# A hand-ordered opening: c spread by DMA, the norm's sums taken per token, GpSimd out, loads reordered, and the first two matmul passes split by features

## The chip, the core and the metric

The kernel runs on one NeuronCore of a Trainium2 chip. The metric is device microseconds (us) of one launch; lower is better. The engines run their own instruction streams and meet at semaphores: TensorE (PE: matmuls, and weight loads as PEld), VectorE (DVE), ScalarE (ACT), GpSimd (POOL), and SyncE (SP), which here only issues DMAs.

## The reference, cut to what matters

A transformer block with conditioning from a vector, then two more layers. Only the very beginning matters here: two token sets of 256 (x and ctx), their modulation vectors, the first norm and the first half of the first feed-forward (D = 1024, D_FF = 2816):

```python
mod_lat = silu(c) @ w_mod + b_mod            # 9 pieces of 1024: shift, scale, gate, ...
mod_ctx = silu(c_ctx) @ w_mod + b_mod
h  = modulate(rms_norm(x,  norm1_g), ml[0], ml[1])    # h * (1 + scale) + shift
hc = modulate(rms_norm(ctx, norm1_g), mc[0], mc[1])
a, b = split(h @ ffn1_w_in)                  # the first matmuls; then silu(a) * b, @ ffn1_w_out
# ... attention, conv, a second feed-forward, an mLSTM / stick-breaking layer, a pooling layer
```

## The kernel before

Tokens lie transposed: `X[128, 8, 512]` holds feature k*128+p on partition p, ctx in columns 0 to 255 and x in 256 to 511. Every matmul is three matmuls: weights and tokens are split into a high part (`WH`, `XH`) and a rest (`WL`, `XL`), and high*high, rest*high and high*rest are summed in PSUM (L758 to L760). Weights come in chunks of 512 KB into a ring of six slots `W`; SP issues the loads of `plan.loads` in one fixed order, each as soon as the slot's last reader is done (L692 to L701). Per chunk ACT writes `WH` (L1140) and DVE writes `WL` (L1471); that is a `split` step.

A class `Plan` writes one list of steps, and each engine walks this list in order and does its part of every step. A `gemm` is one pass: 256 output columns of a weight matrix, two chunks of four features each (`ck` steps, 24 matmuls of 512 columns each), into two of four PSUM tiles; the passes "fa1" and "fb1" of one column pair go together (silu(a) * b). `start()` writes the opening, the steps ahead of the first pass:

- `cb`: PE spreads c and c_ctx over the partitions, a matmul with one row of ones (L786), and ACT writes their silu to `AC0` and `AC1` (L1147).
- `mp`: one 128-feature piece of the scale row, a product and a sum along 1024 elements on DVE for each of the two vectors (L1522). Eight pieces are wanted before the last features are normed.
- `mm`, `mt`: two features pairs' worth (256 values) of the shift row on PE (L795, eight matmuls), copied out by ACT (L1153), turned by PE (L802), stored by DVE as `MOD`, and `AM` = (1 + scale) * gain with it (L1487, L1489).
- `st`, `sr`: the sums of squares: eight squares of 128x512 on ACT (L985), added up by POOL (L955), then a matmul with ones (L724), a square root on ACT (L1162), a reciprocal on DVE (L1497); POOL then writes `XR` = X times that row (L960).
- `fn`: for two features k and both token sets, the tokens' high and low parts: DVE multiplies and adds (L1507), ACT rounds (L995), DVE takes the rest (L1330).

The loads stand in the order scale 0, scale 1, shift 0 (two loads), scale 2, scale 3, shift 1, and so on, and then the passes. The first pass takes features 0 to 7, then the second does.

## Time and profile before

| | us |
|---|---|
| median of 3 runs (1452.12 to 1455.38) | 1454.88 |
| the profiled execution | 1454.74 |
| its span, first to last instruction | 1452.9 |
| TensorE busy in the span | 1351.9 (93%) |
| VectorE busy | 925.9 (64%) |
| ScalarE busy | 644.9 (44%) |
| GpSimd busy | 45.6 (3%) |

Busy time is an average over stages with different limits, so the opening is read by itself: first in stretches of time, then instruction by instruction on each engine. The granted clock is TensorE's, as a share of 2.4 GHz (1.00) with 1.2 GHz as its lower level (0.50). A float32 matmul shows as two records each with its own weight load; a "half" below is one of them.

### The profile page before, as it was taken

Reading aid. Unit: us, or ns where it says so; the run is one execution under the profiler, and the core shown is the slowest. Engines: PE = TensorE matmul, PEld = TensorE weight load, DVE = VectorE, ACT = ScalarE, POOL = GpSimd, SP = SyncE. Lnnn points to the kernel's source line nnn. Section 1 sums busy time; section 2 is a strip of 40 time slices with the busy share of each in tenths; the row PEclk is TensorE's granted clock in tenths of the full one; section 3 lists DMA queues with packets and bytes.
Section 4 is the critical chain, followed back from the end, with each engine's and each line's share of the span. In section 5 each row is a group of like instructions: output and inputs, shape, how many; then the busy total and the mean of one; then the engine's idle time right before and its main releaser. Section 6 shows DMA issues by size and latency. Waiting matters only on the chain.

```text
span 1452.9 us, 22846 instructions
## 1 busy us (share of the span) xinstructions
PE 1351.9 (93%) x9116; PEld 1212.2 (83%) x9116; DVE 925.9 (64%) x1459; ACT 644.9 (44%) x1005; POOL 45.6 (3%) x42
## 2 busy tenths in 40 slices
PE   4599999999997999999989999899999999889996
PEld 1378888888885789999989999779899998879996
DVE  4665455653447467777877655588776665487864
ACT  2242222222235334545454444565565675455553
POOL 2300000000010000000010000100000000000001
PEclk9699999999998999999999999989899999999998
DMA  7263444543352334366658755547255554536561
GB/s 283 70 215 101 160 142 148 173 131 132 130 165 83 101 110 138 102 217 222 218 197 259 247 186 182 159 122 198 74 146 163 144 152 137 174 100 191 184 199 40
DMA packets 201116, 228.61 MB, mean 157 GB/s; under 512 B 7089, under 2 KB 191665, under 8 KB 201009
## 3 DMA queue, kind: packets, MB, share of 16 engines
q1 hardware_dynamic: 200720, 226.85, 49.5%
q8 instruction: 72, 1.18, 0.3%
q14 instruction: 34, 0.28, 0.1%
q10 hardware_dynamic: 290, 0.30, 0.1%
HBM read 226.07 MB, written 1.05 MB: 156 GB/s over the span
## 4 chain that ended last, share of the span: by engine, by line
PE 59%; DVE 6%; ACT 2%; issue 2%; DMA 0%; ACTq 0%; SPq 0%; DVEq 0%
PE P L758 16%; PE P L759 16%; PE P L760 16%; PE P L764 1%; PE P L765 1%; PE P L766 1%; DVE WL L1471 1%; PE P L853 1%; PE P L841 1%; ACT WH L1140 1%; DVE TS L1322 1%; DVE RS L1558 1%; PE P L830 1%; PE P L846 0%; DVE X L1587 0%
## 5 line engine op out<-in xcount | busy, mean ns | idle before, releaser
L1471 DVE TENSOR_TENSOR WL<-W,WH 128x1024 fp32r<-128x1024 f32 x358 | 430.7, 1216 | 304.4 <-ACT WH L1140 303.5
L758 PE MATMUL P<-XH,WH 128*128 128x256 f32 (+1 forms) x1808 | 563.7, 312 | 21.9 <-DVE XL L1332 9.0
L759 PE MATMUL P<-XL,WH 128*128 128x256 f32 (+1 forms) x1808 | 550.7, 305 | 0.0
L760 PE MATMUL P<-XH,WL 128*128 128x256 f32 (+1 forms) x1808 | 550.3, 304 | 0.0
L1140 ACT ACTIVATE WH<-W 128x1024 fp32r<-128x1024 f32 x358 | 368.6, 1042 | 252.2 <-PE P L760 147.8
L758 PEld LDWEIGHTS P<-XH,WH 128*128 128x128 f32 x1808 | 346.1, 191 | 48.8 <-issue 21.0
L759 PEld LDWEIGHTS P<-XL,WH 128*128 128x128 f32 x1808 | 346.1, 191 | 20.3 <-issue 2.9
L760 PEld LDWEIGHTS P<-XH,WL 128*128 128x128 f32 x1808 | 345.8, 191 | 17.0
L758 PE MATMUL P<-GH,WH 128*128 128x512 f32 (+1 forms) x352 | 119.8, 340 | 0.0
L760 PE MATMUL P<-GH,WL 128*128 128x512 f32 (+1 forms) x352 | 119.0, 338 | 0.0
L759 PE MATMUL P<-GL,WH 128*128 128x512 f32 (+1 forms) x352 | 119.0, 338 | 0.0
L1522 DVE CUSTOM_DVE_ANT_0 W<-W,AC,V 128x1024 f32<-128x1024 f32 x64 | 83.9, 1311 | 0.0
L955 POOL TENSOR_TENSOR SQ<-SQ 128x512 f32<-128x512 f32 (+1 forms) x30 | 35.0, 1167 | 1372.9 <-ACT SQ L985 1371.4
L1020 ACT ACTIVATE GH<-TS 128x512 fp32r<-128x512 f32 (+1 forms) x44 | 22.7, 525 | 115.5 <-DVE TS L1348 115.4
L758 PEld LDWEIGHTS P<-GH,WH 128*128 128x128 f32 x352 | 66.3, 188 | 8.2 <-issue 0.5
L759 PEld LDWEIGHTS P<-GL,WH 128*128 128x128 f32 x352 | 66.3, 188 | 8.2 <-issue 0.5
L760 PEld LDWEIGHTS P<-GH,WL 128*128 128x128 f32 x352 | 66.3, 188 | 7.7
L1348 DVE TENSOR_TENSOR TS<-TS,P 128x512 f32<-128x512 f32 (+1 forms) x44 | 23.9, 552 | 73.4 <-PE P L760 73.3
L1014 ACT ACTIVATE TS<-P 128x512 f32<-128x512 f32 (+1 forms) x44 | 21.5, 490 | 77.7 <-PE P L760 77.6
L1522 DVE CUSTOM_DVE_ANT_0 JK<-W,AC,V 128x1024 f32<-128x1024 f32 x32 | 41.7, 1304 | 17.6 <-ACT AC L1147 16.5
L764 PE MATMUL P<-WH,XH 128*128 128x256 f32 x160 | 46.5, 290 | 0.0
L765 PE MATMUL P<-WL,XH 128*128 128x256 f32 x160 | 45.7, 286 | 0.0
(273 smaller groups left out, 1815.7 us busy)
## 6 DMA issues: line engine op xcount, KB each, us to landing
W<-in_ffn_w_in SPq DMA_DIRECT2D x88, 512.0 KB, 5.3
W<-in_w_in_ab SPq DMA_DIRECT2D x72, 512.0 KB, 3.7
W<-in_w_modt SPq DMA_DIRECT2D x64, 512.0 KB, 4.1
W<-in_w_in SPq DMA_DIRECT2D x52, 512.0 KB, 3.6
W<-in_ffn_w_out SPq DMA_DIRECT2D x40, 512.0 KB, 4.7
W<-in_w_in_c SPq DMA_DIRECT2D x32, 512.0 KB, 4.4
W<-in_w_out_ab SPq DMA_DIRECT2D x16, 512.0 KB, 3.4
W<-in_w_out_c SPq DMA_DIRECT2D x16, 512.0 KB, 3.9
```

The costliest lines, as they stand in the source:

```text
L758: pe.matmul(o, h[:, k, c], xh[:, kk, a:b], start=kk == 0, stop=False)
L759: pe.matmul(o, h[:, k, c], xl[:, kk, a:b], start=False, stop=False)
L760: mm = pe.matmul(o, l[:, k, c], xh[:, kk, a:b], start=False, stop=kk == gm.nk - 1)
L764: pe.matmul(o, xh[:, kk, c], h[:, k, :], start=kk == 0, stop=False)
L765: pe.matmul(o, xh[:, kk, c], l[:, k, :], start=False, stop=False)
L955: pool.tensor_tensor(SQ[:, 0, 0:n], SQ[:, 0, 0:n], SQ[:, 1 + (k - 1) % 2, 0:n], ALU.add) \
L1014: act.activation(TS[:, f % NS, 0:n], ps, ACT.Silu).then_inc(S["sil" + kind[2]], 1)
L1020: act.activation(GH[m][:, f % 12, :], TS[:, f % NS, 0:n], ACT.Copy).then_inc(S[f"hh{m}"], 1)
L1140: act.activation(h, a, ACT.Copy).then_inc(S["wh"], 1)
L1348: dve.tensor_tensor(TS[:, f % NS, 0:n], TS[:, f % NS, 0:n], ps, ALU.mult).then_inc(S[f"hm{m}"], 1)
L1471: dve.tensor_tensor(l, a, h.bitcast(F32), ALU.subtract).then_inc(S["wl"], 1)
L1522: td = dve.tensor_tensor_reduce(a if v == s.c - 1 else JK[:, :, :], a, (AC0, AC1)[v][:, :, :], 1.0, vec("bmod", 8 * g + k), ALU.mult, ALU. ...
```

## The change

- c and c_ctx are spread by two DMAs that read one 4 KB row for each of 128 partitions into `AC0` and `AC1`, ahead of all else on SP's queue; ACT takes their silu in place. The PE matmuls of `cb` are gone, and `mp` waits for the vector it reads.
- The sums of squares are taken per token: ACT squares x, then ctx (four squares of 128x512 each, into buffers that stay); PE loads each 128x128 square as the weight and multiplies it with one column of ones (step `s1`, 16 matmuls for each token set). The square root and the reciprocal then work on 128x2, and a diagonal matrix and a matmul with ones spread the result back over the partitions (step `r1`, each token set by itself).
- POOL has no part in the first norm. `fn` reads X and that row directly; the shift is added where the high and the low part are made.
- The loads stand in the order scale 0 to 3, shift 0, the first pass's features 0 to 3, shift 1, the second pass's features 0 to 3, scale 4 and 5, shift 2, scale 6 and 7, shift 3, and then the two passes' features 4 to 7. ctx is loaded behind scale 2.
- The first two passes are written out in `start()`: both take features 0 to 3 (with steps `part`), ahead of scales, shifts and norm of features 4 to 7, and then features 4 to 7.

The core of the diff (the new step code on PE and ACT; DVE's `fn` reads `X` with `base` and `low` of the later norms):

```diff
+        for k in range(2):
+            scales(k)
+        self.step("s1", a=0)
+        for k in range(2, 4):
+            scales(k)
+        self.step("s1", a=1)
+        self.step("r1", a=0)
+        self.step("r1", a=1)
...
+        b = shifts(0)
+        split(0)
+        self.step("mt", a=0, bank=b)
         self.step("fn", a=0)
-        self.split_to(16)
+        split(1)
+        b = shifts(1)
+        self.step("mt", a=1, bank=b)
         self.step("fn", a=1)
...
+        scales(4)
+        scales(5)
+        self.part(ga, 0, chunks[0])
+        b = shifts(2)
+        self.step("mt", a=2, bank=b)
         self.step("fn", a=2)
+        self.part(gb, 0, chunks[1])
+        split(2)
+        scales(6)
+        scales(7)
+        b = shifts(3)
+        self.step("mt", a=3, bank=b)
         self.step("fn", a=3)
+        split(3)
+        self.part(ga, 4, chunks[2])
+        n = self.chunks[chunks[3]][0]
+        self.split_to(n + 1)
+        self.part(gb, 4, chunks[3])
+        self.split_to(n + LOOK)
...
+            for v, acc in enumerate((AC0, AC1)):
+                sp.dma_start(acc[:, :, :], w["cc"][v:v + 1, :].partition_broadcast(128)
+                             .rearrange("p o (t c) -> p (o t) c", t=4)).then_inc(SI[4 + 2 * v], 16)
...
+                elif s.kind == "s1":
                     pe.wait_ge(SI[1], 16)
...
+                    for i in range(4):
+                        pe.wait_ge(S["sq"], 4 * s.a + i + 1)
+                        for k in range(2):
+                            for t in range(2):
+                                c = 256 * k + 128 * t
+                                mm = pe.matmul(P[:, s.a, t:t + 1], squares(s.a, i)[:, c:c + 128], con("one", 0, 1),
+                                               start=i + k + t == 0, stop=i == 3 and k == 1 and t == 1)
+                    mm.then_inc(S["on"], 1)
+                elif s.kind == "r1":
+                    pe.wait_ge(S["ra"], 3 * s.a + 2)
+                    pe.matmul(NB[:, 0:256] if s.a == 0 else P[:, 2, 0:256], con("one"),
+                              TS[:, 5, 256 * s.a:256 * s.a + 256], start=True, stop=True).then_inc(S["rb"], 1)
...
-                if name == "s1":
-                    pool.wait_ge(S["ri"], 2)
-                    for k in range(8):
-                        pool.tensor_tensor(XR[:, k, :], X[:, k, :], RS[:, 0, :], ALU.mult).then_inc(S["xr"], 1)
...
+                elif s.kind == "r1":
+                    v = s.a
+                    act.wait_ge(S["on"], v + 1)
+                    act.activation(RT[:, 2 * v:2 * v + 2], P[:, v, 0:2], ACT.Sqrt, scale=1.0 / D, bias=con("eps")) \
+                        .then_inc(S["ra"], 1)
+                    act.wait_ge(S["ri"], v + 1)
+                    for t in range(2):
+                        dg = act.activation(TS[:, 5, 256 * v + 128 * t:256 * v + 128 * t + 128], con("id"), ACT.Copy,
+                                            scale=RT[:, 2 * v + t:2 * v + t + 1])
+                    dg.then_inc(S["ra"], 1)
+                    act.wait_ge(S["rb"], v + 1)
+                    cp = act.activation(RS[:, 0, 256 - 256 * v:512 - 256 * v], NB[:, 0:256] if v == 0 else P[:, 2, 0:256],
+                                        ACT.Copy)
+                    cp.then_inc(S["sr" if v else "ra"], 1)
```

TensorE's first instructions before (CR holds c, SC the silu of c, SQ the squares, RS the shift row that is turned):

```order
L786 MATMUL P<-CR,C 128x512 x4
L795 MATMUL P<-W,SC 2x256 x16
L802 MATMUL P<-C,RS 128x2 x2
L724 MATMUL P<-SQ,C 128x512 x3
L795 MATMUL P<-W,SC 2x256 x8
L802 MATMUL P<-C,RS 128x2 x2
L795 MATMUL P<-W,SC 2x256 x8
L802 MATMUL P<-C,RS 128x2 x4
L758 MATMUL P<-XH,WH 128x512
```

and now (L853 the sums with the squares in TS and SQ, L858 the spreading with the diagonal in TS, L867 the shift, L874 its turn, L823 the first pass):

```order
L853 MATMUL P<-C,TS 128x1 x16
L853 MATMUL P<-C,SQ 128x1 x12
L853 MATMUL P<-C,TS 128x1 x4
L858 MATMUL P<-TS,C 128x256 x2
L867 MATMUL P<-W,SC 2x256 x8
L874 MATMUL P<-C,RS 128x2 x2
L867 MATMUL P<-W,SC 2x256 x8
L874 MATMUL P<-C,RS 128x2 x2
L823 MATMUL P<-XH,WH 128x512
```

The sums and the spreading of both token sets stand ahead of the first shift, and two shifts instead of four stand ahead of the first pass.

VectorE before, from the last scale piece ahead of the norm (JK, W and MOD are the scale pieces) to the first weight split:

```order
L1522 ISA W,MOD<-W,AC,V 128x1024
L1522 ISA MOD 128x1
L1497 RECIPROCAL RS<-RS 128x256 x2
L1487 TENSOR_TENSOR MOD<-P,V 128x2
L1489 SCALAR_TENSOR_TENSOR AM<-MOD,V 128x2
L1487 TENSOR_TENSOR MOD<-P,V 128x2
L1489 SCALAR_TENSOR_TENSOR AM<-MOD,V 128x2
L1507 TENSOR_SCALAR TS<-XR,AM,MOD 128x256 x2
L1330 TENSOR_TENSOR XL<-TS,XH 128x256
L1507 TENSOR_SCALAR TS<-XR,AM,MOD 128x256
L1330 TENSOR_TENSOR XL<-TS,XH 128x256
```

and now, from the same place:

```order
L1594 ISA W,MOD<-W,AC,V 128x1024
L1594 ISA MOD 128x1
L1572 RECIPROCAL AM<-AM 128x2 x2
L1548 TENSOR_TENSOR WL<-W,WH 128x1024
L1564 TENSOR_TENSOR MOD<-P,V 128x2
L1566 SCALAR_TENSOR_TENSOR AM<-MOD,V 128x2
L1564 TENSOR_TENSOR MOD<-P,V 128x2
L1566 SCALAR_TENSOR_TENSOR AM<-MOD,V 128x2
L1399 SCALAR_TENSOR_TENSOR TS<-X,AM,RS 128x256 x2
L1409 SCALAR_TENSOR_TENSOR XL<-TS,MOD,XH 128x256
L1399 SCALAR_TENSOR_TENSOR TS<-X,AM,RS 128x256
```

Four scale pieces instead of six stand between the loads and the first norm, the reciprocals have 2 columns, and the first weight split stands ahead of the norm. The norm reads X and RS itself.

SyncE's first DMAs now (before, `cc` was one small DMA of ACT's queue, and the order was two `w_modt`, x, ctx, two `w_mod`, two `w_modt`):

```order
L754 DMA AC<-in_cc 128x1024 x2
L760 DMA W<-in_w_modt 128x1024 x2
L762 DMA X<-in_xt 128x8x256
L760 DMA W<-in_w_modt 128x1024
L764 DMA X<-in_ctxt 128x8x256
L760 DMA W<-in_w_modt 128x1024
L760 DMA W<-in_w_mod 128x1024 x2
L760 DMA W<-in_ffn_w_in 128x4x256
```

`w_modt` are scale loads, `w_mod` shift loads, `ffn_w_in` the passes' weights; what stands ahead of x is 1 MB more than before.

## Rows read from the trace of the kernel before

**Rows 1.** Busy time by stretch: us from:to, length, engines' busy (instructions), clock, DMA.

```profile
core 0: us, PE busy (x) PEld busy (x) DVE busy (x) ACT busy (x) POOL busy (x), PEclk, DMA share, GB/s
...
80.00:440.00 360.00, 360.00 (x1545) 289.89 (x1544) 188.17 (x256) 95.81 (x118) 6.50 (x5) 1.00 0.44 144
```

**Rows 2.** Timeline of PE: start, length, line, operands, count, idle before and releaser.

```profile
8.57 7.19 PE L786 MATMUL P<-CR,C 1*128 1x512 f32 x8 [8.57 <-DMA C<-in_consts]
...
15.69 5.63 PE L795 MATMUL P<-W,SC 128*2 128x256 f32 x16
...
38.47 5.43 PE L724 MATMUL P<-SQ,C 128*128 128x512 f32 x6 [10.79 <-POOL SQ L955]
...
43.83 3.62 PE L795 MATMUL P<-W,SC 128*2 128x256 f32 x16
...
78.04 0.50 PE L758 MATMUL P<-XH,WH 128*128 128x512 f32 x1 [0.28 <-DVE XL L1330]
...
92.61 0.39 PE L760 MATMUL P<-XH,WL 128*128 128x512 f32 x1
92.84 0.40 PE L758 MATMUL P<-XH,WH 128*128 128x512 f32 x1
```

**Rows 3.** Timeline of VectorE, the opening.

```profile
16.55 1.28 DVE L1522 CUSTOM_DVE_ANT_0 JK<-W,AC,V 128x1024 f32<-128x1024 f32 x1 [16.55 <-ACT AC L1147]
...
19.22 1.28 DVE L1522 CUSTOM_DVE_ANT_0 JK<-W,AC,V 128x1024 f32<-128x1024 f32 x1 [0.17 <-DVE MOD L1522]
...
27.72 0.16 DVE L1487 TENSOR_TENSOR MOD<-P,V 128x2 f32<-128x2 f32 x1 [0.65 <-PE P L802]
...
29.20 2.28 DVE L1522 CUSTOM_DVE_ANT_0 W<-W,AC,V 128x1024 f32<-128x1024 f32 x1
...
50.92 2.55 DVE L1507 TENSOR_SCALAR TS<-XR,AM,MOD 128x256 f32<-128x256 f32 x2 [1.25 <-POOL XR L960]
```

**Rows 4.** SP's issues of x and ctx (timeline), then issues and landing times of transfers.

```profile
1.64 0.43 SPq L698 DMA_DIRECT2D X<-in_xt  x1
2.11 1.16 SPq L699 DMA_DIRECT2D X<-in_ctxt  x1
...
W<-in_w_branch_attn SPq DMA_DIRECT2D x8, 512.0 KB, 5.9
...
X<-in_xt SPq DMA_DIRECT2D x1, 1024.0 KB, 8.7
X<-in_ctxt SPq DMA_DIRECT2D x1, 1024.0 KB, 11.2
```

**Rows 5.** Timeline of PE's weight loads, the turns of the shift row.

```profile
27.08 0.52 PEld L802 LDWEIGHTS P<-C,RS 2*128 2x128 f32 x4 [0.44 <-issue]
...
64.69 0.92 PEld L802 LDWEIGHTS P<-C,RS 2*128 2x128 f32 x4 [12.72 <-ACT RS L1153]
```

**Rows 6.** Matmuls that read C until 60 us: ns min/median/max; then stretches with the clock.

```profile
L786 PE MATMUL P<-CR,C x8: 1056/1056/1216, 8.6 to 14.7; 1*128 1x512 f32 x8
...
L724 PE MATMUL P<-SQ,C x6: 1001/1057/1219, 38.5 to 42.9; 128*128 128x512 f32 x6
...
38.00:40.00 2.00, 1.53 (x2) 0.83 (x3) 0.00 (x0) 0.63 (x1) 0.41 (x1) 0.50 0.39 160
...
44.00:46.00 2.00, 2.00 (x11) 0.78 (x10) 0.00 (x0) 1.95 (x2) 0.00 (x0) 1.00 0.00 0
...
64.00:66.00 2.00, 1.31 (x5) 1.30 (x6) 1.85 (x5) 1.58 (x3) 0.00 (x0) 0.50 0.04 8
```

**Rows 7.** Timeline of ACT.

```profile
27.47 1.65 ACT L985 ACTIVATE SQ<-X 128x512 f32<-128x512 f32 x3
...
47.48 0.37 ACT L1153 ACTIVATE RS<-P 2x256 f32<-2x256 f32 x1 [1.52 <-PE P L795]
...
52.22 0.42 ACT L995 ACTIVATE XH<-TS 128x256 fp32r<-128x256 f32 x1 [4.37 <-DVE TS L1507]
...
94.30 1.99 ACT L1140 ACTIVATE WH<-W 128x1024 fp32r<-128x1024 f32 x2
```

**Rows 8.** Timeline of VectorE in the second norm, and the page's group of splits.

```profile
445.96 0.88 DVE L1322 SCALAR_TENSOR_TENSOR TS<-X,AM,RS 128x256 f32<-128x256 f32 x2
...
449.46 0.48 DVE L1332 SCALAR_TENSOR_TENSOR XL<-TS,MOD,XH 128x256 fp32r<-128x256 f32 x1
...
L1471 DVE TENSOR_TENSOR WL<-W,WH 128x1024 fp32r<-128x1024 f32 x358 | 430.7, 1216 | 304.4 <-ACT WH L1140 303.5
```

More of the change, by code:

```diff
@@ L259, in mod_part, with pass_over, part @@
         self.prog.append(run)
-    def start(self, parts):
+    def pass_over(self, kind, i, wt, nk, c0, cols):
+        gm = Gemm(kind, i, 0, wt, 0, nk, c0, cols, True, kind == "fa1")
+        return gm
+    def part(self, gm, k0, j):
+        if k0 == 0:
+            base = len(self.tile_end)
+            gm.tiles = [base, base + 1]
+            for _ in gm.tiles:
+                self.tile_end.append(0)
+                self.tile_free.append(self.up(self.EVICT[gm.kind]))
+        last = k0 + 4 == gm.nk
+        for t in gm.tiles if last else (0,):
+            self.marks += 1
+            if last:
+                self.tile_end[t] = self.marks
+        self.chunk_end[j] = self.marks
+        self.step("ck", gemm=gm, k0=k0, nk=4, chunk=j, a=int(last))
@@ L263, in start, with scales, split @@
+    def start(self, scale, shift, fa, fb, chunks):
         banks = []
-        def scales(c):
-            for j in range(2):
-                self.step("mp", a=1, b=2 * c + j, c=2, load=parts[c][j])
+        ga, gb = fa, fb
+        def scales(k):
+            self.step("mp", a=1, b=k, c=2, load=scale[k])
         def shifts(c):
             b, f = self.bank(("mv", c + 1))
-            banks.append(b)
-            self.step("mm", a=c, load=parts[c][2], bank=b, free=f)
-        def turn(c):
-            self.step("mt", a=c, bank=banks[c])
+            self.step("mm", a=c, load=shift[c], bank=b, free=f)
+            return b
+        def split(i):
+            self.split_to(self.chunks[chunks[i]][0])
@@ L309, in build, with shift_load, weights @@
         w, LAT, ALL = self.w, (256, 512), (0, 512)
-        parts = []
-        for c in range(4):
-            parts.append([self.mod_load(1, 2 * c + j) for j in range(2)])
+        scale, shift, chunks = {}, {}, []
+        fa = self.pass_over("fa1", 0, w["ffn1_w_in"], 8, 0, ALL)
+        fb = self.pass_over("fb1", 0, w["ffn1_w_in"], 8, DFF, ALL)
+        def shift_load(c):
             for r in range(2):
                 src = w["w_mod0"][2 * c + r].rearrange("p (t c) -> p t c", t=4)
-                parts[c].append(self.load(src, 4, [("mm", 2 * c + r + 1)]))
-        self.call(self.start, parts)
+                n = self.load(src, 4, [("mm", 2 * c + r + 1)])
+                shift.setdefault(c, n)
+        def weights(gm, k0):
+            src = gm.w[k0 * 128:k0 * 128 + 512, gm.c0:gm.c0 + 256].rearrange("(t p) c -> p t c", p=128)
+            chunks.append(self.chunk(src, 4))
+        for k in range(4):
+            scale[k] = self.mod_load(1, k)
+        shift_load(0)
+        weights(fa, 0)
+        shift_load(1)
+        weights(fb, 0)
+        for k in range(4, 6):
+            scale[k] = self.mod_load(1, k)
+        shift_load(2)
+        for k in range(6, 8):
+            scale[k] = self.mod_load(1, k)
+        shift_load(3)
+        weights(fa, 4)
+        weights(fb, 4)
+        self.call(self.start, scale, shift, fa, fb, chunks)
         self.mod_list([2, 3, 4, 5])
@@ L440, in ffn @@
         for f0, f1 in ((0, 12), (12, 22)):
-            for f in range(f0, f1, 2):
+            for f in range(2 if n == 1 and f0 == 0 else f0, f1, 2):
                 self.gemm(f"fa{n}", f, win, 0, 8, f * 128, cols, first=f == 0)
@@ L585, in build_program @@
         SW = [ctx.enter_context(nc.semaphore(f"s_w{i}")) for i in range(WR)]
-        SI = [ctx.enter_context(nc.semaphore(f"s_in{i}")) for i in range(6)]
+        SI = [ctx.enter_context(nc.semaphore(f"s_in{i}")) for i in range(7)]
         def sbuf(st, name, shape, dt=F32):
@@ L804, in _ @@
                     mm.then_inc(S["mt"], 1)
-                elif s.kind == "st":
-                    for i in range(3):
-                        ones("s1", i)
                 elif s.kind == "norm":
@@ L1144, in _ @@
                     for v, acc in enumerate((AC0, AC1)):
[L1145 to L1148 removed]
+                        act.wait_ge(SI[4 + 2 * v], 16)
+                        act.activation(acc[:, :, :], acc[:, :, :], ACT.Silu).then_inc(S["cb"], 1)
                 elif s.kind == "mm":
```

88 lines of the change are left out of this document (30 added, 58 removed).

## The prediction, made before the changed kernel ran

> **What bounds the kernel now.** I read the stretches first. From 80 to 440 us TensorE is busy for 360.0 of 360.0 us at clock 1.00 [rows 1]: once the first passes run, nothing but matmul work sets the pace for 360 us, and whatever the opening saves arrives whole at 440 us. So one number measures the change: the start of the third pass. Before it is 92.84 us [rows 2]. Then I read each engine's timeline through the opening. PE works on other things, waits and runs at the lower clock until the matmul at 78.04, the last one that waited; from there 63 of the 96 matmuls of the first two passes are left and run at 0.233 us each (92.84 less 92.61) [rows 2]. What keeps PE waiting is a chain: c spread on PE from 8.57 to 15.7 [rows 2], scale pieces from 16.55 [rows 3], sums that POOL adds up until PE may start at 38.47 [rows 2], and a norm that waits for POOL's product at 50.92 and, beside POOL, takes 2.55 us for two instructions [rows 3].
>
> **The change part by part.** I follow the new order to the start of the third pass. Times are us from the span's start.
>
> *c and the loads.* PE's 7.19 us and the wait for them go; ACT's silu of two 128x1024 tiles comes in (about 1.0 each by the casts of that shape, 1.99 for two [rows 7]). In place of it 1 MB more stands ahead of x. Ahead of x's end there are now 3 MB on SP's queue, as many as stood ahead of ctx's end before, and that landed at 2.11 + 11.2 = 13.3 [rows 4]. So x lands at 13.3 instead of 1.64 + 8.7 = 10.3. The 1 MB between these two took 3.0 us, 350 GB/s; scale 2 and ctx (1.5 MB) follow at 17.8, scale 3 at 19.3, shift 0 at 22.3. Reading one row 128 times is in no row. The bounds: it can hardly be faster than the 350 GB/s of the other loads by more than some tenths of a us in all, and if each of the two took the 5.9 us of the slowest 512 KB group [rows 4], one after the other, it would cost 11.8 in place of 3.0, or 8.8 more. I take 3.0, since these are whole 4 KB rows into 128 partitions like the scale loads beside them.
>
> *Scale pieces.* One takes 19.22 - 16.55 = 2.67 for both vectors [rows 3]. Without POOL the pieces that took 2.28 for a half beside it [rows 3] fall back to 1.28. Four pieces, each behind its load, end at 19.3 + 2.7 = 22.0 and wait for nobody after that.
>
> *Sums.* ACT's squares come at 0.55 (1.65 for three [rows 7]), the first at 13.9. PE has 16 matmuls for each token set, 32 halves, each a weight load of 128 columns and one moving column, so 64 in all. The nearest rows are the turns of the shift row, four halves with 128 weight columns and two moving ones: 0.52 at the higher clock, 0.92 at the lower (0.50 from 64 to 66) [rows 5, 6]. That is 0.13 or 0.23 each, 8.3 or 14.7 in all. Which level? The clock view says 1.00 until 28 us, but the matmuls of L786 take 1056 ns, as long as L724's 1057 at a granted 0.50 [rows 6]. So PE starts at the lower level, and 7.19 us of L786 without a gap did not raise it, since the next 16 halves still took 5.63 against 3.62 later [rows 2]; the 5.43 us of L724 did raise it (0.50 at 38, 1.00 at 44) [rows 6]. No row has the sums' shape. L786 shows that matmuls without a gap can stay at the lower level, and nothing ahead of the sums can have raised it; I take the lower level for all 64: 13.9 + 14.7 = 28.6.
>
> The Trainium skill, "TensorE: Matmul & The Clock Gate", Part 1, says that the throttled clock is the default and that sustained activity releases it; by that rule the sums would be raised on their way, which is a rival below. The same page, section "LDWEIGHTS (loading the stationary operand)", gives 107 ns for 128 columns whatever the rows; 64 of them are an estimated 6.8 us, and the sum would be 1436.4 by it; the turns show 130 and 230 ns, and I go by them.
>
> *Spreading back.* The first token set's root, reciprocal and diagonals are done while PE sums the second. Left: a matmul of 256 columns (half of L724's shape, 0.9 for its two halves), its copy (0.4), the second set's root (0.2), reciprocal (0.2), two diagonals (0.6), matmul (0.9), and five handovers of 0.1. No row has these small shapes; each ACT one is above zero and not over the 0.42 of 128x256 [rows 7], so the sum lies between 2.3 and 4.2; I take 3.7: 32.3.
>
> *Shift 0.* It stands behind all that on PE. 16 halves after a spell at the lower clock: 5.63 as before; 3.62 if raised [rows 2]. That gives 37.9. Copy 0.37 [rows 7], turn 0.6, four small DVE instructions 0.3 (the first is 0.16 [rows 3]), handovers: 1.6. The norm starts at F = 39.5. The first split is done by then.
>
> *Norm and first parts, from F.* One `fn` is four multiplies and four rests. In the second norm the same instructions run from 445.96 to 449.46 + 0.4 = 449.86 for the fourth [rows 8], 3.9. Features 0 and 1: F + 3.9. The second split stands next on DVE and waits for ACT's cast behind the roundings, F + 5.6 (1.0 [rows 7] and 1.2 [rows 8]). Shift 1's values (0.3), features 2 and 3: F + 9.8. On PE the first part needs all four, then has 15 matmuls left, 3.5, and only then comes shift 2, 3.6, with copy and turn 1.2: F + 18.1. DVE's scales 4 and 5 (5.3, F + 15.1) are hidden by that. So DVE waits 3.0 here. Values 0.3, features 4 and 5: F + 22.3. Third split, whose load was issued behind scale 5 and lands by F + 20.5: F + 24.0. Scales 6 and 7: F + 29.3; meanwhile PE does the second part (5.6) and shift 3 with its turn (4.8), F + 28.5, hidden with 0.8 to spare. Values, features 6 and 7: F + 33.5.
>
> *To the third pass.* 39 matmuls are left (3 + 12 + 24), 9.1 and 0.1: F + 42.7 = 82.2. The third pass's second chunk is split behind the second pass's eviction: its cast can start 94.30 - 92.84 = 1.5 after that pass [rows 2, 7], is done 1.0 later and its rest 1.2 after that, 3.7 against 5.6 of matmul work. It is hidden; without that cover it would cost 3.7.
>
> **Sum.** 92.84 - 82.2 = 10.6 saved. The profiled execution took 1454.74, 0.14 under the median of the runs; 1454.88 - 10.6 = 1444.3.
>
> **The rivals.**
>
> *The clock rises during the sums.* If the sums raise it as L724 did, after 5.4 us, these are at 0.23 (23 halves), 41 follow at 0.13: 13.9 + 10.7 = 24.6, 4.0 less. Spreading saves 0.9 more, shift 0 runs at 3.62, 2.0 less: F = 32.6, 17.5 saved, 1437.4. For it: L724 is the row that reads squares too, and it did raise it. Against: L786's 7.19 us without a rise.
>
> *The spread reads are slow* (the other side). All partitions read the same 4 KB, so one part of memory may serve all 128 reads. The two DMAs stand ahead of everything and x lands later by just as much. They have 3.0 us in my sum; the gain is gone at 13.6 us (77 GB/s), and it is slower by over 0.2% from 16.5 us (64 GB/s); at 50 GB/s they take 21 and the time is 1462. For it: no row shows such a read. Against: 8 KB of the same data caused no wait that the trace names.
>
> *It does not carry.* If the cover of the third pass's split fails or a load comes behind a slot's release that I put too early, two to three more waits of 3 to 4 us would leave little of the gain: 1453. Against: the margins of 0.8 to 1.9 us above.
>
> **How the numbers follow.** Forecast 0.56 (1440 to 1449.5, by the bounds of spreading and of the reads), clock rises 0.26 (1435.5 to 1440), slow reads 0.12, not carried 0.06. About 0.2% (2.9 us) is what a measurement of this kernel can tell from no change. Faster: 0.56 + 0.26 + 0.04 + 0.01 = 0.87. Same: 0.03 + 0.04 = 0.07. Slower: 0.05 + 0.01 = 0.06. The range 1435.5 to 1450 holds the first two cases and leaves out most of the others.
>
> **What would show it.** Right: x's squares start near 13.3; the sums L853 take about 14.7 us on PE with a granted clock of 0.50; the norm's first L1399 at about 39.5; the last L1409 of the opening at about 73; DVE idle some 3 us ahead of features 4 and 5; the third pass at about 82; PE without a gap from there to about 430. Wrong: a clock of 1.00 in the second half of the sums (then 75), squares that start after 17 (slow reads), or PE idle after the third pass's start.

## The result, and the profile after

| | before | after |
|---|---|---|
| median, 13 runs of each, us | 1453.51 (1450.47 to 1457.05) | 1445.66 (1441.50 to 1451.25) |
| ratio, 95% interval | | 0.995 (0.9938 to 0.9962) |
| the profiled execution, us | 1454.74 | 1445.66 |
| its span, us | 1452.9 | 1443.9 |

Faster by 0.5%. The ratio makes a gain of 7.3 us, with 5.5 to 9.0 as its interval (0.995, 0.9962 and 0.9938 of 1453.51); the two spans differ by 9.0. The time was forecast at 1444.3 and the gain at 10.6, so the time came out 1.4 us later than forecast and the gain some 3 us smaller.

First TensorE's timeline of the changed kernel (start and length in us, engine, line, operands, count, in brackets how long it stood idle before and what ended that). It answers to [rows 2]:

```profile
13.72 6.96 PE L853 MATMUL P<-C,TS 128*128 128x1 f32 x32 [13.72 <-ACT TS L1223]
20.54 5.26 PE L853 MATMUL P<-C,SQ 128*128 128x1 f32 x24
25.66 1.85 PE L853 MATMUL P<-C,TS 128*128 128x1 f32 x8
27.37 1.20 PE L858 MATMUL P<-TS,C 128*128 128x256 f32 x2
30.12 1.22 PE L858 MATMUL P<-TS,C 128*128 128x256 f32 x2 [1.55 <-ACT TS L1233]
31.27 5.12 PE L867 MATMUL P<-W,SC 128*2 128x256 f32 x16
...
43.85 0.60 PE L874 MATMUL P<-C,RS 2*128 2x2 f32 x4 [2.85 <-ACT RS L1215]
...
83.08 0.39 PE L823 MATMUL P<-XH,WH 128*128 128x512 f32 x1
```

The first three rows are the sums of squares: 64 halves from 13.72 to 27.4 with no pause between them, 0.217 us each (6.96 / 32). The last row is the third pass, 9.76 us earlier than the 92.84 of [rows 2].

Next VectorE, the rows that answer to [rows 3] (the last is the eviction of the second pass's second tile, VectorE's reading of the finished sums from PSUM, which I use below to compare kernels; in the kernel before it stands at 93.04):

```profile
19.73 1.28 DVE L1594 CUSTOM_DVE_ANT_0 W<-W,AC,V 128x1024 f32<-128x1024 f32 x1
...
37.78 1.22 DVE L1548 TENSOR_TENSOR WL<-W,WH 128x1024 fp32r<-128x1024 f32 x1 [8.44 <-ACT WH L1204]
...
39.32 0.88 DVE L1399 SCALAR_TENSOR_TENSOR TS<-X,AM,RS 128x256 f32<-128x256 f32 x2
...
57.37 0.16 DVE L1564 TENSOR_TENSOR MOD<-P,V 128x2 f32<-128x2 f32 x1 [3.42 <-PE P L874]
...
72.14 0.48 DVE L1409 SCALAR_TENSOR_TENSOR XL<-TS,MOD,XH 128x256 fp32r<-128x256 f32 x1 [0.18 <-ACT XH L1062]
...
83.27 0.69 DVE L1425 TENSOR_TENSOR TS<-TS,P 128x512 f32<-128x512 f32 x1 [2.11 <-PE P L825]
```

The norm starts at 39.32, VectorE waits 3.42 for the turned shift rows of features 4 and 5, and the last low part of the opening starts at 72.14. The second row is the first weight split. It stands ahead of the norm on VectorE and waits for ScalarE's high part, which starts only when shift 0 has been copied out:

```profile
36.43 0.37 ACT L1215 ACTIVATE RS<-P 2x256 f32<-2x256 f32 x1 [4.67 <-PE P L867]
36.71 1.04 ACT L1204 ACTIVATE WH<-W 128x1024 fp32r<-128x1024 f32 x1
```

Last, stretches (us from:to, length, TensorE's busy time and instructions, granted clock, DMA share, GB/s):

```profile
44.00:46.00 2.00, 2.00 (x8) 0.65 0.74 268
46.00:48.00 2.00, 1.65 (x4) 0.50 0.68 246
72.00:74.00 2.00, 1.63 (x4) 0.50 1.00 346
74.00:76.00 2.00, 2.00 (x7) 0.67 0.94 329
84.00:430.00 346.00, 345.69 (x1482) 1.00 0.43 145
```

From 84 to 430 TensorE is busy for 345.69 of 346.00 us at clock 1.00, nearly as before [rows 1]. In the first four rows the granted clock falls to 0.50, TensorE's lower level, behind its waits at 41.0 to 43.85 and at 69.3 to 71.2, and part of the first passes runs there.

The landings of the transfers that answer to [rows 4] (issue, count, KB each, median us to landing):

```profile
AC<-in_cc SPq DMA_DIRECT2D x2, 512.0 KB, 5.4
X<-in_xt SPq DMA_DIRECT2D x1, 1024.0 KB, 10.0
X<-in_ctxt SPq DMA_DIRECT2D x1, 1024.0 KB, 11.3
```

### The profile page after: what moved, and what is told of

Same layout as the page of the kernel before. It is cut to its first block, busy times and chain, and to the rows that moved or that the text cites. A ratio compares the mean times of both kernels' runs of the same rounds, so it can differ in the third digit from the quotient of the medians.

```text
span 1443.9 us, 22946 instructions
## 1 busy us (share of the span) xinstructions
PE 1350.8 (94%) x9170; PEld 1217.2 (84%) x9170; DVE 916.1 (63%) x1459; ACT 647.1 (45%) x1011; POOL 26.0 (2%) x29
## 4 chain that ended last, share of the span: by engine, by line
PE 56%; DVE 7%; ACT 3%; DMA 2%; issue 2%; POOL 0%; SPq 0%; ACTq 0%; DVEq 0%; POOLq 0%
PE P L823 15%; PE P L824 15%; PE P L825 15%; DMA W<-in_ffn_w_in 2%; PE P L829 1%; PE P L830 1%; PE P L831 1%; DVE WL L1548 1%; ACT WH L1204 1%; PE P L922 1%; PE P L910 1%; DVE TS L1399 1%; DVE RS L1630 1%; PE P L899 1%; DVE XL L1409 1%
## 5 line engine op out<-in xcount | busy, mean ns | idle before, releaser
L823 PE MATMUL P<-XH,WH 128*128 128x256 f32 (+1 forms) x1808 | 563.5, 312 | 24.0 <-DVE XL L1409 11.9
L823 PEld LDWEIGHTS P<-XH,WH 128*128 128x128 f32 x1808 | 344.8, 191 | 52.7 <-issue 21.0
L823 PE MATMUL P<-GH,WH 128*128 128x512 f32 (+1 forms) x352 | 119.9, 341 | 0.3 <-DVE WL L1548 0.3
L823 PEld LDWEIGHTS P<-GH,WH 128*128 128x128 f32 x352 | 66.3, 188 | 8.9 <-DVE WL L1548 0.7
L1024 POOL TENSOR_TENSOR SQ<-SQ 128x256 f32<-128x256 f32 (+1 forms) x25 | 25.8, 1032 | 1394.6 <-ACT SQ L1050 1393.7
```

The source lines that it names most:

```text
L823: pe.matmul(o, h[:, k, c], xh[:, kk, a:b], start=kk == 0, stop=False)
L1024: pool.tensor_tensor(SQ[:, 0, 0:n], SQ[:, 0, 0:n], SQ[:, 1 + (k - 1) % 2, 0:n], ALU.add) \
```

## The experiments

Each is a copy of the changed kernel with the edit shown. Ratios are to runs of the kernel before made beside them, whose medians lie between 1453.1 and 1454.8, so kernels are compared by ratios; "tile" is the start of the eviction named above, 93.04 before and 83.27 after.

| | median, us | ratio (95% interval) | norm starts | last low part | tile |
|---|---|---|---|---|---|
| changed kernel | 1445.66 | 0.995 (0.9938 to 0.9962) | 39.32 | 72.14 | 83.27 |
| e9_same: the same again | 1447.10 | 0.9958 (0.9942 to 0.9973) | 39.88 | 73.90 | 83.84 |
| e1_whole: passes not split | 1453.52 | 0.9995 (0.9981 to 1.0008) | 39.85 | 74.02 | 90.39 |
| e2_c_by_pe: c spread by TensorE | 1452.37 | 0.9991 (0.9977 to 1.0004) | 44.33 | 78.05 | 87.99 |
| e3_warm: work ahead of the sums, then a pause | 1446.81 | 0.996 (0.9945 to 0.9976) | 39.31 | 72.13 | 84.89 |
| e10_warm2: work ahead of the sums, no pause | 1443.44 | 0.9926 (0.9908 to 0.9945) | 37.30 | 71.62 | 82.46 |
| e4_ones: sums in another form | 1435.08 | 0.9877 (0.986 to 0.9895) | 30.19 | 64.45 | 74.39 |
| e5_shift2: one shift step earlier | 1444.82 | 0.9944 (0.9929 to 0.9959) | 38.71 | 69.85 | 81.33 |
| e6_both: e4 and e5 | 1433.40 | 0.9862 (0.9844 to 0.9879) | 29.41 | 61.40 | 72.88 |
| e7_mt1: e4, and a copy earlier | 1436.73 | 0.9883 (0.9865 to 0.9902) | 29.43 | 63.40 | 73.34 |
| e11_fill: e6, with work in a wait | 1432.60 | 0.9855 (0.9837 to 0.9873) | 29.30 | 60.29 | 70.24 |
| e12_fill_warm: e11, and work ahead of the sums | 1431.77 | 0.9846 (0.983 to 0.9862) | 29.11 | 60.19 | 71.67 |

### The same kernel again: how far does the gain move on its way?

No edit. Expected:

> The changed kernel itself, unaltered, a second time. It asks how far the lags at later places move from execution to execution: in the first pair of traces the third pass is 9.8 us earlier than before, the second norm 9.2, the third 7.8, the fourth 6.6, the layer after 9.7 and the end 9.1. If this is what executions do, the same places give other lags here, by up to 1.5 us, and the time is 1444 to 1447; if the change itself costs something in the attention stage, the lags repeat: 7.8 and 6.6 at the third and the fourth norm.

Measured: 1447.10, and the lags behind the kernel before, worked out from VectorE's reciprocals of the later norms, are:

| us earlier than before at | tile | 2nd norm | 3rd norm | 4th norm | next layer's norm | last norm |
|---|---|---|---|---|---|---|
| in the kernel before, that is | 93.04 | 444.17 | 744.40 | 942.35 | 1269.13 | 1442.59 |
| changed kernel | 9.77 | 9.19 | 7.77 | 6.58 | 9.66 | 9.09 |
| the same again | 9.20 | 8.29 | 7.20 | 4.68 | 7.01 | 3.75 |
| e4_ones | 18.65 | 17.94 | 17.72 | 18.20 | 17.68 | 17.69 |
| e11_fill | 22.80 | 21.93 | 22.07 | 22.28 | 22.72 | 22.63 |

What follows: the gain at the end moves between executions of one kernel. The same code comes to the last norm 9.1 us earlier than before in one execution and 3.75 in another (a late one: its time is 1450.99, the highest of this kernel's eight), from openings that differ by 0.6. That is more than the 1.5 I had allowed. One pair of traces therefore gives the gain at the third pass well and the gain at the end badly; for the end only the 13 runs count.

The other question was whether something is lost on the way each time, and the traces say yes. From the second norm to the fourth the changed kernel loses 2.6 us in the first execution and 3.6 in the second, and the traces of the five other kernels below with one-column sums (e1, e2, e3, e10, e5) lose 2.3 to 3.0. Of the five with the sums of e4_ones four lose 0.4 or nothing and e12_fill_warm loses 2.1. In five of the seven most of it is back at the next layer's norm. From the tile to the last norm all seven traces with one-column sums lose, 0.7 to 5.5 us and 2.4 in the mean; of the other five two gain. All of this is measured against one execution of the kernel before. Nothing here shows why an opening that is done by 84 us should matter at 700; the cause stays open.

Whether the clock falls in the opening also moves. Behind a wait of 1.91 us the changed kernel ran at 0.50; the same kernel, behind the same wait, did not:

```profile
72.98 0.50 PE L823 MATMUL P<-XH,WH 128*128 128x512 f32 x1 [1.90 <-DVE XL L1409]
```
```profile
72.00:74.00 2.00, 0.97 (x3) 1.00 1.04 389
74.00:76.00 2.00, 1.56 (x7) 1.00 1.04 373
```

In the first pass's features 0 to 3 it was the other way round: here the clock was 0.50 from 46 to 52, in the first execution only to 48, so VectorE waited 4.62 us for the shift rows of features 4 and 5 instead of 3.42.

### The passes not split

```diff
-        self.part(gb, 0, chunks[1])
         split(2)
...
         self.split_to(n + 1)
+        self.part(gb, 0, chunks[1])
         self.part(gb, 4, chunks[3])
```

> Undoes one part: the second pass takes features 0 to 3 only when the first pass has taken all eight, so TensorE has 63 matmuls instead of 39 behind the last low part. Theory (the split is worth what it hides): 24 matmuls at 0.233 us each = 5.6 us more behind the last low part, which itself stays at 72.1 to 72.6 us; third pass at about 88.7 instead of 83.07, time 1451.3, about 5.6 us above the changed kernel. Rival (VectorE's chain of scales and norms sets the third pass anyway, or the loads do): no difference, 1445.7. Second rival: without the second pass's matmuls at 57 to 62 us TensorE reaches the shift rows of features 6 and 7 sooner, the last low part comes up to 3 us sooner, and the difference is 2.6 us or less.

Measured: the tile at 90.39, 7.1 us later; 1453.52, nothing left of the gain. TensorE, with the wait in brackets, and the clock around it:

```profile
73.10 0.80 PE L823 MATMUL P<-XH,WH 128*128 128x512 f32 x1 [5.76 <-DVE XL L1409]
```
```profile
72.00:74.00 2.00, 0.90 (x2) 0.50 1.07 376
74.00:76.00 2.00, 2.00 (x5) 0.50 1.01 367
```

What follows: the theory holds and is a little small. Of the 7.1 us, 1.9 are a later last low part (74.02 against 72.14), and 5.2 are the 24 matmuls that now stand behind it (5.6 at 0.233). The 1.9 are not the split itself: in this execution the clock stayed at 0.50 for longer in the first part, from 46 to 52 and not only to 48, so the shift rows behind it came later and VectorE waited 4.78 instead of 3.42. The unaltered e9_same has the same stretch and the same last low part (73.90); against it the tile is 6.5 us later. The second rival (the last low part earlier) did not occur: TensorE made the last shift rows as soon as it could, but VectorE was still at work on the scale pieces that it takes ahead of them.

### c spread by TensorE again

```diff
-                sp.dma_start(acc[:, :, :], w["cc"][v:v + 1, :].partition_broadcast(128)
-                             .rearrange("p o (t c) -> p (o t) c", t=4)).then_inc(SI[4 + 2 * v], 16)
...
+                            pe.matmul(P[:, 2 * v + c, :], con("one", rows=1), CR[:, v, 512 * c:512 * c + 512], start=True,
+                                      stop=True).then_inc(S["cp"], 1)
...
+            act.dma_start(CR[:, :, :], w["cc"].rearrange("(o v) c -> o v c", o=1)).then_inc(SI[4], 16)
...
-                        act.wait_ge(SI[4 + 2 * v], 16)
+                            act.wait_ge(S["cp"], 2 * v + c + 1)
```

> Undoes one part: c and c_ctx come as one row each and are spread by matmuls with a row of ones, as in the kernel before; the rest stays. Theory A (only TensorE's 7.2 us ahead of the sums count): sums begin at 15.8 instead of 13.7, first norm at 41.4 instead of 39.3, time 1447.7. Theory B (ScalarE takes its steps in order, so the squares wait behind the silu of the last spread part at about 16.6 and a table load of 1.3): squares begin at about 18.2 instead of 12.95, sums end at about 32.7 instead of 27.4, first norm at 44.6, time 1451.0. Rival (the scale pieces, ready at 25 instead of 21.0, set the norm): under 1 us, since the sums end later than that.

TensorE's sums, then ScalarE's last silu and what stands behind it:

```profile
19.39 6.96 PE L861 MATMUL P<-C,TS 128*128 128x1 f32 x32 [2.81 <-ACT TS L1234]
```
```profile
16.61 0.60 ACT L1220 ACTIVATE AC<-P 128x512 f32<-128x512 f32 x1 [1.11 <-PE P L851]
17.22 1.28 ACT L1231 ACT_TABLE_LOAD   x1
18.52 0.20 ACT L1231 ACTIVATE RS<-C 128x1 f32<-128x1 f32 x1
18.63 2.17 ACT L1234 ACTIVATE TS<-X 128x512 f32<-128x512 f32 x4
```

Measured: squares at 18.63 (18.2 expected by theory B), norm at 44.33 (44.6), tile 4.7 us later, 1452.37 (1451.0). What follows: theory B. The spread by DMA is worth 4 to 5 us at the third pass (4.7 against the changed kernel's first execution, 4.2 against the second). The sums start 5.7 us later (19.39 against 13.72). Half of that is TensorE's own time, since it spreads c until 16.6; the other 2.81 it waits for the squares, which stand on ScalarE behind a silu that waits for TensorE's fourth matmul. The two DMAs that replace it landed 5.4 us after issue in the changed kernel, so they were not slow.

### Is it the clock? Work ahead of the sums

e3_warm has 12 such matmuls, e10_warm2 has 22; the edit of the first:

```diff
                     pe.wait_ge(SI[1], 16)
+                    for i in range(12 if s.a == 0 else 0):
+                        pe.matmul(P[:, 3, 0:128], con("one"), con("id"), start=True, stop=True)
                     for i in range(4):
```

> Adds 12 matmuls of 128 columns (128 rows, float32, into an unused bank) from 8.6 us, when the constants land, to about 13.9, ahead of the sums of squares. They compute nothing that is used. Theory A (the sums hold the clock where they find it): granted clock 1.00 in the sums, which then cost about 0.11 us for each half instead of 0.216 and end at about 20.5, behind the last square at 19.4, instead of 27.4; shift 0 takes 3.6 instead of 5.1; first norm at about 30 and time about 1436 to 1438. Theory B (64 matmuls of one column cannot keep the clock up): it falls back within the sums, they end between 24 and 27.6, and the time is 1443 to 1446. Theory C (these matmuls do not raise it either): nothing moves, 1445.7 to 1446.2.

> The changed kernel with 22 instead of 12 matmuls of 128 columns (results unused) from 7.7 us, so that TensorE has no pause of 1.74 us ahead of the sums of squares, as it had with 12 of them, where the clock was 1.00 until 14.0, 0.3 us into the sums, and 0.50 behind that. Theory A (the pause let it fall): granted clock 1.00 in the sums of x, 0.11 instead of 0.216 us a half, sums end at about 20.5 and the first norm at about 31, time about 1438. Theory B (weight loads with matmuls of one column cannot hold the clock): it falls within the sums all the same, they end at 26 to 27.8, time 1445 to 1447.

With 12 of them there is a pause from 12.0 to 13.75. The stretches of e3_warm:

```profile
11.00:12.00 1.00, 1.00 (x10) 1.00 1.14 369
12.00:13.00 1.00, 0.01 (x1) 1.00 1.00 380
13.00:14.00 1.00, 0.25 (x3) 1.00 1.07 376
14.00:15.00 1.00, 1.00 (x7) 0.52 1.09 347
```

The clock, raised by these matmuls, is at 0.52 from 14 to 15, behind the pause, and the sums took as long as without them (until 27.2). Theory A is out. The end of the sums fits theory B (24 to 27.6), but with the pause just ahead it does not tell whether the pause or the sums brought the clock down; 1446.81 is a little above the times of both B and C. With 22 there is no pause. TensorE's rows of e10_warm2, then its stretches:

```profile
7.70 7.55 PE L849 MATMUL P<-C 128*128 128x128 f32 x44 [7.70 <-DMA C<-in_consts]
15.08 3.63 PE L855 MATMUL P<-C,TS 128*128 128x1 f32 x32
18.57 4.40 PE L855 MATMUL P<-C,SQ 128*128 128x1 f32 x24
22.83 1.85 PE L855 MATMUL P<-C,TS 128*128 128x1 f32 x8
```
```profile
18.00:19.00 1.00, 1.00 (x11) 1.00 1.01 401
19.00:20.00 1.00, 1.00 (x9) 0.77 1.00 396
20.00:21.00 1.00, 1.00 (x6) 0.50 1.06 365
```

The sums of x run at the upper level, 0.113 a half (3.63 / 32); then, with TensorE in the sums and no pause anywhere, the clock falls between 19 and 20. The last eight halves take 0.231 each, as they do without the extra work (1.85 / 8).

What follows: neither theory alone. The clock can be up when the sums begin, and they run at twice the speed then; but the clock fell on the way, in a stretch in which TensorE did nothing but one-column matmuls and their weight loads. The sums end 2.8 us earlier (24.5), the norm starts at 37.30, 2.0 earlier, and little of that arrives: the first pass's matmuls ran at the lower level until about 50, the shift rows of features 4 and 5 came only at 56.85 (57.37 without), and VectorE waited 4.91 for them. Tile 0.8 us earlier. What the opening's first half saved was given back at the next wait.

### The sums in another form

```diff
-                            for t in range(2):
-                                c = 256 * k + 128 * t
-                                mm = pe.matmul(P[:, s.a, t:t + 1], squares(s.a, i)[:, c:c + 128], con("one", 0, 1),
-                                               start=i + k + t == 0, stop=i == 3 and k == 1 and t == 1)
+                            mm = pe.matmul(P[:, s.a, 0:256], con("one"), squares(s.a, i)[:, 256 * k:256 * k + 256],
+                                           start=i + k == 0, stop=i == 3 and k == 1)
...
+                    act.activation(RS[:, 0, 256 - 256 * v:512 - 256 * v], P[:, v, 0:256], ACT.Sqrt, scale=1.0 / D,
+                                   bias=con("eps")).then_inc(S["sr" if v else "ra"], 1)
...
+                    r = RS[:, 0, 256 - 256 * v:512 - 256 * v]
+                    dve.wait_ge(S["sr" if v else "ra"], 1)
+                    dve.reciprocal(r, r).then_inc(S["ri"], 1)
```

The root and the reciprocal on 128x2, the diagonals, the spreading matmul and the copy of step `r1` are gone.

> Changes the form of the sums: a matrix of ones is the stationary operand and the squares move through it, 8 matmuls of 256 columns for each token set; the sums then stand on all partitions, the root and the reciprocal take 128x256, and the diagonal and the spreading matmuls are gone. Theory A (it was the form of the sums that held the clock down, as 128x512 matmuls with ones raised it in the kernel before after 5.4 us): 0.9 us each for about 6 of them, then 0.45; sums end at 23.5 to 25, reciprocals at 26 to 27, shift 0 at the upper level in 3.6, first norm at 29 to 31, time 1436 to 1438. Theory B (the clock stays low in the opening whatever runs, until about 35 us): sums end at 28.5, shift 0 ends at 33.6 without the spreading of 3.7 ahead of it, first norm at 35.2, time about 1441.6. Rival on the other side (the reciprocals of 128x256, 1.75 each on VectorE, or the loads behind the scale pieces become the limit): first norm at 33 or later at the upper clock.

TensorE of e4_ones:

```profile
14.11 6.16 PE L851 MATMUL P<-TS,C 128*128 128x256 f32 x16 [14.11 <-ACT TS L1217]
20.11 2.75 PE L851 MATMUL P<-SQ,C 128*128 128x256 f32 x12
22.70 1.03 PE L851 MATMUL P<-TS,C 128*128 128x256 f32 x4
23.65 3.62 PE L861 MATMUL P<-W,SC 128*2 128x256 f32 x16
```

and VectorE's wait for the shift rows of features 4 and 5:

```profile
49.68 0.16 DVE L1549 TENSOR_TENSOR MOD<-P,V 128x2 f32<-128x2 f32 x1 [4.86 <-PE P L868]
```

Measured: sums end at 23.65 instead of 27.4, a half of 256 columns at 0.229 in ctx's first three squares (2.75 / 12), against 0.385 in x's (6.16 / 16), on whose way the clock rose; shift 0 at 3.62, the upper level; norm at 30.19 instead of 39.32; 1435.08. What follows: theory A. In all four kernels that start this form at the lower level (e4, e6, e7, e11) the clock rose in the sums, with 2.75 us for these twelve halves each time; in none of the seven traces with one-column sums did it rise there. Of 9.1 us at the norm, 3.7 are the sums, 3.9 the spreading that is gone (27.37 to 31.27), 1.5 the faster shift 0 (5.12 less 3.62). The 3.7 are the clock's: theory B has this form, at the lower level throughout, end at 28.5, later than the one-column sums. The reciprocals of 128x256 lie in VectorE's free time. And the 9 us arrive at the third pass (8.9) and at the end (ratio 0.9877 against 0.995, about 10.6 us, give or take some 3).

### The waits that are left

In e5_shift2 the shift rows of features 4 and 5 go ahead of the first pass; e6_both has this and the sums of e4_ones; e7_mt1 has the sums of e4_ones and only ScalarE's copy of shift 1 and its turn ahead of the second split.

```diff
         scales(5)
-        self.part(ga, 0, chunks[0])
         b = shifts(2)
         self.step("mt", a=2, bank=b)
+        self.part(ga, 0, chunks[0])
```

> The changed kernel with one thing moved: TensorE makes and turns the shift rows of features 4 and 5 ahead of the first pass's features 0 to 3, not behind them. Theory (VectorE's wait of 3.42 us for that turn at 53.9 to 57.4 is on the path to the third pass): the wait goes, the norm of features 4 and 5 starts at about 54.3 instead of 57.8, a wait of about 1.4 for the next turn stays, the last low part comes about 2.7 us earlier, third pass at 79 to 80.5 instead of 83.07, time about 1442.5. Rival (the rows' load lands too late, at 46 or after, and TensorE stands still for it and has the first pass's matmuls left at the end): third pass at 82 to 84, no difference.

> The sums with ones as the stationary operand, and the shift rows of features 4 and 5 ahead of the first pass's features 0 to 3. Theory: beside the kernel with only the first of the two (1435.08, third pass's second tile at 74.39, VectorE waiting 4.86 for that turn at 44.8 to 49.7) the wait goes; TensorE waits for the rows until about 36.8 and has only matmuls from there, the last low part comes at about 60.5 instead of 65, the tile at about 69, time 1429.5 to 1431. Rival (TensorE's late start on the first pass is given back at the end): 1434 to 1436.

> The sums with ones as the stationary operand, and ScalarE's copy of the shift rows of features 2 and 3, with their turn, ahead of the split of the second weight chunk instead of behind it. Theory (ScalarE's order of steps holds TensorE back by 2.86 us at 31.9 to 34.7, and the clock falls behind that): first pass begins about 1.1 us earlier; if the clock then stays at 1.00 through the first pass its 24 matmuls take 5.6 instead of 9.7, VectorE's wait of 4.86 shrinks to 1 or 2, and the time is about 1431; if the clock falls all the same, 1434. Rival (VectorE sets it anyway): 1435.

The step that moved, on TensorE, in e5_shift2 and then in e6_both:

```profile
44.03 5.00 PE L867 MATMUL P<-W,SC 128*2 128x256 f32 x16
```
```profile
35.67 4.92 PE L861 MATMUL P<-W,SC 128*2 128x256 f32 x16 [1.13 <-DMA W<-in_w_mod]
```

In both, VectorE's wait for features 4 and 5 is gone and the last low part comes 2.3 us (69.85) and 3.1 us earlier (61.40); the tile gains 1.9 and 1.5 us, less than the 2.6 to 5.4 expected, and the times (1444.82, 1433.40) cannot be told from those without the move. One reason is in the two rows: 5.00 and 4.92 instead of 3.62, since TensorE had waited 2.86 and 2.85 us just ahead and ran at 0.50 again. Two more are in the traces: VectorE now waits 1.93 and 1.83 us for the high part of the third weight chunk, for whose load ScalarE had waited; and in e6_both the clock fell once more at 62 to 65, where e4_ones had kept it, which took back 1.5 of the 3.1 us. In e7_mt1 the first pass starts at 33.55, earlier as meant, but the clock falls at 35.0 all the same, behind TensorE's wait of 1.90 us ending at 33.0 and just ahead of its next, 2.15 us for the norm of features 2 and 3: 1436.73, no gain.

The clock in that wait is what e11_fill tries, with 12 matmuls of unused results:

```diff
                         mm.then_inc(S["mm"], 1)
+                    for i in range(12 if s.a == 1 else 0):
+                        pe.matmul(P[:, 3, 0:128], con("one"), con("id"), start=True, stop=True)
```

> The kernel with both improvements (sums with ones as the stationary operand; shift rows of features 4 and 5 first), and 12 matmuls of 128 columns with unused results in TensorE's wait of 2.85 us at 31.1 to 33.95. Theory (the clock fell in the next step, shift 2 at 4.92 instead of 3.62, because TensorE had stood still): shift 2 takes 3.6, the third pass's second tile comes 1.0 to 1.3 earlier than 72.88, at 71.6 to 71.9; time 1431.5 to 1433, which the time alone may not tell from 1433.4. Rival: the load of the rows, not the clock, sets this place, and nothing moves.

> The same, with 22 matmuls of unused results also from 7.7 us, ahead of the sums. Theory: the sums of x with ones as the stationary operand then run at the upper clock, behind the squares: x's end at 17.6 instead of 19.5, ctx's at 19.9 instead of 22.9, and shift 0, whose load lands at about 22.3, becomes what sets the norm; first norm at 28.5 instead of 29.4, third pass at 70.7 or so, time 1430.5 to 1432.5. Rival (the clock falls in the sums as with one column): x's sums take 5.7 or more, and the time is that of the kernel without these matmuls.

TensorE of e11_fill, and the whole rest of its opening:

```profile
30.92 2.95 PE L865 MATMUL P<-C 128*128 128x128 f32 x24
33.84 0.60 PE L870 MATMUL P<-C,RS 2*128 2x2 f32 x4
34.84 3.61 PE L861 MATMUL P<-W,SC 128*2 128x256 f32 x16 [0.39 <-DMA W<-in_w_mod]
```
```profile
34.00:70.00 36.00, 31.93 (x140) 1.00 0.62 211
```

Shift 2 takes 3.61, the clock is 1.00 from 34 to 70, and the tile comes at 70.24, 2.6 us earlier than in e6_both. Of these, 1.1 are there at the last low part, as expected for the faster shift 2. The other 1.5 are the later fall of the clock, which e6_both had and this execution had not; that the extra work prevents it is not shown, since e12_fill_warm has the same extra work and the fall. In e12_fill_warm the sums of x also run at the upper level from their start:

```profile
15.57 3.62 PE L853 MATMUL P<-TS,C 128*128 128x256 f32 x16
```

but they start 1.9 us later (the extra work lasts until 15.7), so the norm starts only 0.2 us earlier, and in its execution the clock was at 0.50 from 62 to 64, behind TensorE's wait of 2.06 us ending at 59.3: tile 71.67. The median of this kernel, 1431.77, is the lowest of all, 0.9846 of the kernel before and by the ratios about 15 us under the changed kernel; against e11_fill and e6_both their intervals overlap, so which of the three is best stays open.

## Why the prediction was right, and where it was off

| step | forecast | measured |
|---|---|---|
| x's squares start | 13.3 | 12.95 |
| last scale piece done | 22.0 | 21.0 |
| sums done | 28.6 | 27.4 |
| shift 0 starts on TensorE | 32.3 | 31.27 |
| shift 0 takes | 5.63 | 5.12 |
| from its end to the norm | 1.6 | 2.9 |
| norm starts (F) | 39.5 | 39.32 |
| VectorE waits ahead of features 4 and 5 | 3.0 | 3.42 (4.62 in e9_same) |
| last low part done | 73.0 | 72.6 |
| from there to the third pass | 9.2 | 10.5 (9.3 in e9_same) |
| third pass starts | 82.2 | 83.08 |
| saved there | 10.6 | 9.8 |
| saved at the end | 10.6 | 9.1 in the two traces, 7.3 (5.5 to 9.0) over the runs |

*The chain up to the norm* came out within 0.2 us partly by luck. The sums ended 1.2 us early and shift 0 took 0.5 less than forecast, and one step failed the other way: "The first split is done by then." It was not. ScalarE takes the high part of the first chunk only behind its copy of shift 0, from 36.71; VectorE's low part of it runs from 37.78 to 39.0, and the norm's values stand behind that, though the turn was done at 37.5. So 2.9 us lie between shift 0 and the norm where 1.6 was forecast. It is the same in e4_ones (27.27 to 30.19). No run puts the first split ahead of that copy.

*From the norm to the last low part* the steps hold within 0.5 us: 33.3 us where 33.5 was forecast. The wait ahead of features 4 and 5, though, is 3.42 in one execution of this kernel and 4.62 in the other, so part of that closeness is luck too. The choice that decided most, the lower level for all 64 halves of the sums, held: 0.217 a half where 0.23 was taken, 13.7 us where 14.7 was. The sign I named for it does not hold as written: the view shows a granted clock of 1.00 in these sums, which I had called wrong. It shows 1.00 from the start of the trace to 44.6 and tells nothing here; the halves' own 0.217 us is what shows the lower level. (In the kernel before the view reads 1.00 until 30 us, not 28 as I wrote; nothing hangs on that.) The rival in which the clock rises on the way did not occur in the changed kernel, and in e10_warm2 the sums lost the upper level even where they were given it.

This is also where the sentence on the Trainium skill, "TensorE: Matmul & The Clock Gate", Part 1, has to be set against the row. The page says that sustained activity releases the throttled clock; here TensorE is busy with the sums from 13.72 to 27.4 without a pause and stays at 0.217 a half, twice the 0.113 of e10_warm2. The measurement decides: being busy was not enough here, while with the same squares as the moving operand (e4_ones) the clock rose. The same page's section on LDWEIGHTS gives 107 ns for 128 columns; e10_warm2's 0.113 a half agrees with it at the upper level, the sums of the changed kernel (0.217) do not at the lower.

*From the last low part to the third pass* the step that failed in the first execution is the price of the 39 matmuls: 9.1 and 0.1 were taken, all at 0.233 each, and 10.5 was measured (72.6 to 83.08). Six of them ran at the lower level, 2.7 us together instead of 1.4, which is the 1.3 us that is missing. In e9_same none did, and the price was right: 9.3 us (74.4 to 83.65). So this step is open to chance from execution to execution. I had seen how the clock falls behind TensorE's waits in the kernel before [rows 6] and did not carry it to the new wait at 69.3, which my own steps place there (part of the matmuls waits for the last features).

*From the third pass to the end* I claimed that whatever the opening saves arrives whole. [rows 1] shows this to 440 us, and it did nearly: 9.19 of 9.77 is there at the second norm. Behind 440 I had no row and took it for granted, and that term of the sum was too large: the runs give 7.3, with 9.0 as the upper bound, where the third pass gives 9.8, and 0.9958 (about 6.1) where e9_same's tile gives 9.2. The seven traces with one-column sums agree, with 2.4 us lost in the mean between the tile and the last norm. e9_same also shows that this part moves by several us from execution to execution, so the difference of one pair says little. e4_ones and e11_fill carry all but 1.0 and 0.2 of theirs; why the others lose stays open.

*The other rivals.* The spread reads were not slow: 5.4 us to landing where 4.7 was the median of the two loads that stood first on the queue before and 5.9 that of the slowest group of that size [rows 4], and x landed at 2.96 + 10.0 = 12.96. Nothing failed to carry in the sense of the third rival: TensorE waited for no weight load. But the two undone parts show how thin the gain was. Undoing the split costs 6.5 us by the ratios (0.9995 against 0.995), undoing the spread of c 6.0 (0.9991 against 0.995). Each interval is about 2 us wide on either side. At the tile the two are 7.1 and 4.7 of 9.8. So together they are all of the gain or more, as far as parts may be added, and little or nothing is left for the rest of the change (sums per token and spreading back, no work on POOL, the order of loads). No run undoes that rest, so what each of its parts gives or costs is not shown. e4_ones shows only that a third form of the sums, with the same squares and no POOL, is about 10 us better; it does not compare the one-column sums with the form before.

## What to carry to other kernels

Price a matmul by the clock that it will run at, and read that clock from the matmul's own duration and from what TensorE did just ahead; a form that counts few cycles can run at the lower level throughout, as the one-column sums did here. Undo each part of a compound change by itself: here two of five parts were together worth all of the gain or more. When a forecast comes out, compare its steps and not only its end: here a split that was not done in time was hidden by sums that came early. When the gain is a few us, read it at the place where the changed stage ends, in two executions of the same kernel, before believing what the end of one pair says.

## What the runs showed of the hardware that I had not expected

- The clock fell while TensorE was busy without a pause: e10_warm2, 0.77 from 19 to 20 and 0.50 from 20 to 21, in matmuls of one column with a weight load of 128 columns each. In the changed kernel the same sums ran from 13.72 to 27.4 without a rise; in e3_warm and e10_warm2 the clock rose in matmuls of 128 columns ahead of the sums, and in e4_ones in the sums with 256 moving columns.
- Waits of TensorE of 1.7 to 2.9 us were each followed by a stretch at 0.50 in some kernels and not in others: behind the wait of 1.91 us ending at 71.2 the changed kernel shows 0.50, the same kernel in e9_same stays at 1.00 behind its 1.90 us ending at 73.0, and e11_fill behind its 2.26 us ending at 59.4. When the clock comes back also differs: shift 0 took 4.60, 5.12, 5.33 and 5.66 us in kernels with the same opening up to there (e5_shift2, changed kernel, e9_same, e1_whole).
- The granted clock at the beginning of these traces reads 1.00 whatever the level. The sums read 1.00 in the changed kernel and 0.50 in e3_warm, where the clock had changed before them, with the same 0.22 us a half in both; the matmul's own duration is what tells the level there.
- 128 partitions reading one 4 KB row cost little more than an ordinary load of the same 512 KB: 5.4 us to landing (5.6 in e9_same), against 4.7 for the two loads at the same place of the queue in the kernel before.
